# Attention stages of a two-block fp32 transformer kernel: modulation units, PSUM banks, tiles and start times of the heads rearranged

## The chip, the cores and the metric

The kernel runs on 1 core of a Trainium2 chip as one launch. The metric is device time in microseconds (us): the median of several runs. Each run is one execution of the whole program. A difference of some 0.2% (2.5 us) is what a measurement of this kernel can tell from none.

## The reference

Sequence 256, width 1024, batch 1, all in float32. A first block (modulated by a conditioning vector c) is followed by a second one of two layers. What matters of them here:

```python
# first block
mods = silu(c) @ w_ada + b_ada          # nine vectors of 1024: shift, scale, gate x 3
h += 0.5 * gate0 * rmsnorm(swiglu(modulate(rmsnorm(h), shift0, scale0)))        # d_ff 2816
p = modulate(rmsnorm(h), shift1, scale1) @ w_in    # qa ka va | qi ki wi | qb kb vb
oa = rmsnorm(dsa_sparse_attention(qa, ka, va, qi, ki, wi, rel_bias))   # 8 heads of 64, top 64 keys
ob = rmsnorm(stick_breaking_attention(qb, kb, vb))                     # 8 heads of 64
h += gate1 * rmsnorm(concat(oa, ob) @ w_out)
h += 0.5 * gate2 * rmsnorm(swiglu(modulate(rmsnorm(h), shift2, scale2)))
# second block, layer 0
h += diff_attention(rms_norm(h))     # rope, 8 heads: softmax(q1 k1) - lam * softmax(q2 k2), times v
h += sq_relu_mlp(rms_norm(h))        # d_ff 4096
# second block, layer 1
ckv = rms_norm(h) @ w_dkv;  c = rms_norm(ckv[:256]);  k_nope, v = split(c @ w_ukv)
q = rms_norm(rms_norm(h) @ w_dq) @ w_uq       # latent 384, then 8 heads of 128 + 64 (rope)
h += softmax((q_nope k_nope + q_rope k_rope) * scale) v @ w_o
h += sq_relu_mlp(rms_norm(h))
return rms_norm(h)
```

`mods` 6 and 7 are the shift and scale of the third sublayer, the second feed-forward of the first block.

## The kernel before

**Weights as one stream.** All weights come from one array, in an order that `stream_plan` writes out and the host packs accordingly. One load of SyncE's queue brings a 1 MB chunk of two units of 128x1024 (512 KB each) into one of NR = 5 raw slots. `feed()` goes down the plan. It splits a weight unit into a high fp32r part `whi` (ScalarE, L325) and the rest `wlo` (VectorE, L326), in one of NS = 5 slots, and stops when none is free. A raw slot is loaded again when both its units are used up. A unit named `ada` is a piece of `w_ada`: VectorE multiplies it with silu(c) and sums along the row in one instruction (L304), straight from the raw slot, and TensorE has nothing to do with it. `spread(units, mods, wide)` strews the 8 `ada` units of each listed modulation among the units of a stage, `wide` giving the rate.

**Products.** Each product of two float32 operands is three fp32r matmuls on TensorE (high by high, high by low, low by high). `block_T` (through `products`, whose matmuls are L363) makes one unit 24 matmuls of 128x256; `rows_times` makes it 12 of 128x512 into the four long-lived accumulators `fix` (named `pacc` in the rows). Four more PSUM banks (named `ps`) go round by `banks.take()` and `banks.give()`. Both lists are first in, first out.

**Attention beside projections.** While TensorE works through a projection, `Side` runs other parts as Python generators in between: a part issues the instructions up to its next `yield` on all engines. `nudge()` is one turn: it advances one part that is due, or begins one whose condition holds, if fewer than 5 are active. In the first block's `in_t` loop (20 units) and in the `qk` loop of the second block (16 units) a turn comes after 6 matmuls and one at the unit's end, 4 a unit. In the `uq` loop (12 blocks of 9 matmuls) one comes after each 3 matmuls. `yield n` asks for at least n turns before the next step (a bare `yield` 4, in the `uq` loop 3). `step()` is a turn with no product beside it. Every engine takes its instructions in the order in which this Python program wrote them: TensorE stands still at a head's matmul until its operand is there, whatever products stand behind it.

The parts are: `index_part` (the selection of 64 keys: 8 score heads, then 8 rounds of max and match_replace on VectorE, L1001 and L1003); 8 `stick_head`s (three steps); 8 `sparse_head`s (three steps; L1023 adds the bias, L961 is the exponential in `softmax_exp`, `transpose_p` at L932 and L937, `times_v`); two `half_out`s, which normalise 512 columns of the mixed heads and turn them into four "parts" each of the operand `o1` (L1126, L1132), kept in `nhi` and `nlo`; 8 `diff_head`s (four steps) and 8 `latent_head`s (three). In the rows L373 and L376 are the two matmul helpers `put` and `put_last`. A head may begin when it is `ripe`: the projections that it needs were issued at least 2 turns ago. Rope (`roped`, two steps, L1203 to L1214) and the evacuations of queries (L1435 on ScalarE for odd blocks, L1437 on VectorE for even ones) stand beside the heads.

**Ends of the stages.** In an attention stage the four `fix` banks are added to the four round-going ones (`open_fix`). At its end they have to be back before the next product accumulates in them:

```python
        while any(b not in banks.items for b in fix):
            side.step()
        close_fix()
```

The stages after each are `out` (order 4, 5, 6, 7, 0, 1, 2, 3), `o_a` and `o_b`; their `rows_times` gives a turn after each group of three matmuls and steps the side parts until the part that it needs is there.

**The latent stage** before: products `dkv` and `dq`, norm of the kv latent (`low_norm`, L480, L474, L482), product `dkr`, first step of its rope, turning of the normed kv latent (`turn`, L502; parts at L522, L525), second step of the rope, norm of the q latent, products `ukn`, turning of q, products `ukv`, then the `uq` loop with the heads.

## Time and profile before

| | us |
|---|---|
| median of 3 runs | 1258.34 (1258.27 to 1260.52) |
| the profiled execution | 1263.49 |
| its span | 1262.2 |
| TensorE busy in it | 1180.5 (94%), 7782 matmuls |
| VectorE / ScalarE busy | 805.5 (64%) / 619.1 (49%) |
| granted TensorE clock, mean | 0.975 |
| moved by the DMA queues | 231.78 MB, mean 184 GB/s |

How to read it: the profiled execution is 5.15 us above the median and its span 3.9 us above. A clock of 1.00 in a row is 2.4 GHz, 0.50 is 1.2 GHz. Line numbers (L363) are those of the listing. In the trace the stages lie so, in us from the span's start: start 0 to 44.8; first feed-forward 44.8 to 231; value and index projections to 281; `in_t` loop with heads 281 to 384.6; `out` product 395.7 to 426; second feed-forward 435 to 629; `qk` loop with heads 659 to 738; `o_a` to 765; MLP 774 to 950; latent stage 958 to 1045; `o_b` to 1070; MLP 1074 to 1250.

### The profile page before, as it was taken

The page shows a single profiled execution, that of the slowest core. Times are in us where ns is not written, and L with a number is a line of the kernel's source. Part 1 is how long each engine was busy: PE and PEld are TensorE (multiplying, and loading weights), DVE is VectorE, ACT ScalarE, POOL GpSimd, SP SyncE. Part 2 cuts the span into 40 slices and gives each one's busy share as a digit, 9 for nine tenths or more (in the row PEclk, how much of TensorE's full clock was granted, in tenths as well). Part 3 has the DMA queues.
Part 4 walks back from the last instruction along what each step waited for, and adds up shares of the span by engine and source line. Part 5 has one row for each costly group of instructions (what it writes and reads, how often), then busy time and mean ns, then how long its engine had stood idle before and what let it go on. Part 6 is the DMA issues. An engine that isn't in the chain of part 4 may idle for free.

```text
span 1262.2 us, 19662 instructions
## 1 busy us (share of the span) xinstructions
PE 1180.5 (94%) x7782; PEld 1084.0 (86%) x7782; DVE 805.5 (64%) x1343; ACT 619.1 (49%) x1096; POOL 59.1 (5%) x75
## 2 busy tenths in 40 slices
PE   1899999998897999999999889999999879999998
PEld 1799989898896899999989878999998767999997
DVE  6877766659654665655558876565557554655554
ACT  4444454634464544444555545445456443554453
POOL 4000000000000000000002210000000000000000
PEclk8899999989898999999999999999999899999999
DMA  9888777265431366565442223555554304455540
GB/s 382 349 349 302 278 265 266 100 234 203 156 110 67 118 235 221 211 234 184 151 170 102 102 100 133 200 173 196 188 181 173 126 35 150 144 190 194 175 165 34
DMA packets 34011, 231.78 MB, mean 184 GB/s; under 512 B 3704, under 2 KB 5120, under 8 KB 6528
## 3 DMA queue, kind: packets, MB, share of 16 engines
q1 hardware_dynamic: 31952, 226.24, 49.2%
q10 hardware_dynamic: 1968, 4.29, 1.0%
q8 instruction: 62, 1.02, 0.3%
q14 instruction: 29, 0.24, 0.1%
HBM read 229.45 MB, written 1.06 MB: 183 GB/s over the span
## 4 chain that ended last, share of the span: by engine, by line
PE 78%; DVE 13%; ACT 6%; issue 1%; POOL 1%; DMA 1%; DVEq 0%; SPq 0%; ACTq 0%; POOLq 0%
PE ps L363 37%; PE pacc L363 35%; DVE wlo L326 3%; ACT wk L961 2%; DVE raw L304 2%; ACT whi L325 1%; POOL st L468 1%; DVE st L956 1%; PE ps L376 1%; PE pacc L373 1%; PE ps L373 1%; PE pacc L500 1%; PE ps L500 1%; DVE tmp L637 1%; DMA cst<-in_const 1%
## 5 line engine op out<-in xcount | busy, mean ns | idle before, releaser
L326 DVE TENSOR_TENSOR wlo<-raw,whi 128x1024 fp32r<-128x1024 f32 x353 | 430.5, 1225 | 204.6 <-ACT whi L325 198.5
L325 ACT ACTIVATE whi<-raw 128x1024 fp32r<-128x1024 f32 x353 | 369.6, 1054 | 167.6 <-PE pacc L363 91.6
L363 PE MATMUL ps<-nhi,whi 128*128 128x256 f32 x1376 | 399.2, 290 | 20.2 <-DVE wlo L326 17.6
L363 PE MATMUL ps<-nhi,wlo 128*128 128x256 f32 x1376 | 392.3, 285 | 0.0
L363 PE MATMUL ps<-nlo,whi 128*128 128x256 f32 x1376 | 392.3, 285 | 0.0
L363 PEld LDWEIGHTS ps<-nhi,whi 128*128 128x128 f32 x1376 | 266.8, 194 | 26.8 <-ACT whi L325 19.1
L363 PEld LDWEIGHTS ps<-nlo,whi 128*128 128x128 f32 x1376 | 266.8, 194 | 5.0 <-issue 1.0
L363 PEld LDWEIGHTS ps<-nhi,wlo 128*128 128x128 f32 x1376 | 266.6, 194 | 0.0
L363 PE MATMUL pacc<-whi,hhi 128*128 128x512 f32 x440 | 173.1, 393 | 1.1 <-ACT sg L704 1.1
L363 PE MATMUL pacc<-wlo,hhi 128*128 128x512 f32 x440 | 172.5, 392 | 0.0
L363 PE MATMUL pacc<-whi,hlo 128*128 128x512 f32 x440 | 171.2, 389 | 0.0
L704 ACT ACTIVATE sg<-ps 128x256 f32<-128x256 f32 x108 | 41.5, 384 | 180.6 <-PE ps L363 180.4
L363 PEld LDWEIGHTS pacc<-whi,hlo 128*128 128x128 f32 x440 | 82.6, 188 | 18.1
L363 PEld LDWEIGHTS pacc<-whi,hhi 128*128 128x128 f32 x440 | 83.0, 189 | 16.8 <-ACT sg L704 1.4
L363 PEld LDWEIGHTS pacc<-wlo,hhi 128*128 128x128 f32 x440 | 83.0, 189 | 13.1
L706 DVE TENSOR_TENSOR hm<-sg,ps 128x256 f32<-128x256 f32 x108 | 45.4, 421 | 76.4 <-ACT sg L704 76.3
L304 DVE SCALAR_TENSOR_TENSOR raw<-raw,silu_c 128x1024 f32<-128x1024 f32 x72 | 87.7, 1226 | 0.0
L710 DVE TENSOR_TENSOR hlo<-hm,hhi 128x256 fp32r<-128x256 f32 x108 | 45.9, 425 | 52.2 <-ACT hhi L709 52.2
L709 ACT ACTIVATE hhi<-hm 128x256 fp32r<-128x256 f32 x108 | 45.1, 418 | 65.2 <-DVE hm L706 65.2
L468 POOL TENSOR_TENSOR st<-st,mod 128x1 f32<-128x1 f32 (+1 forms) x40 | 25.8, 646 | 1079.7 <-DVE st L658 429.2
L363 PE MATMUL pacc<-whi,nhi 128*128 128x512 f32 (+1 forms) x144 | 57.3, 398 | 7.1 <-DVE nlo L1132 4.3
L363 PE MATMUL pacc<-wlo,nhi 128*128 128x512 f32 (+1 forms) x144 | 55.0, 382 | 0.0
(272 smaller groups left out, 1382.8 us busy)
## 6 DMA issues: line engine op xcount, KB each, us to landing
raw<-in_stream SPq DMA_DIRECT2D x213, 1024.0 KB, 4.9
gates<-in_g_post ACTq DMA_DIRECT2D x3, 512.0 KB, 11.9
h<-in_x SPq DMA_DIRECT2D x1, 1024.0 KB, 7.3
cst<-in_const ACTq DMA_DIRECT2D x1, 1024.0 KB, 8.0
arena<-bias_rows ACTq DMA_DIRECT2D x1, 1024.0 KB, 8.2
out<-tmp SPq DMA_DIRECT2D x4, 256.0 KB, 2.1
silu_c<-in_c_row ACTq DMA_DIRECT2D x1, 512.0 KB, 5.9
arena<-in_final_g SPq DMA_DIRECT2D x1, 512.0 KB, 5.7
```

What stands on the lines that cost most here:

```text
L304: t = dve.do(lambda e: e.scalar_tensor_tensor(src, src, 1.0, silu_c[:, :], ALU.mult, ALU.mult, accum_out=adac[:, 8 * m + k:8 * m + k + 1]) ...
L325: t_hi = act.do(lambda e: e.activation(whi[:, s, :], src, ACT.Copy), arrived, room)
L326: t_lo = dve.do(lambda e: e.tensor_tensor(wlo[:, s, :], src, whi[:, s, :].bitcast(F32), ALU.subtract), arrived, room, t_hi)
L363: return e.matmul(o, lt[a], rh[b], start=start and first, stop=stop and last)
L373: pe.quiet(lambda e: e.matmul(o, lt, rh, start=start, stop=stop), *after)
L468: return pool.do(lambda e: e.tensor_tensor(r, v, ex, ALU.pow), t, t_zero)
L500: tok[c] = pe.do(lambda e: e.matmul(o, a, dg[:, i, :], start=True, stop=True), t, held[c].free)
L704: t = act.do(lambda e: e.activation(sg[:, s, :], up if gate is None else gate, ACT.Relu if gate is None else ACT.Silu), tk)
L706: t = dve.do(lambda e: e.tensor_tensor(hm[:, s, :], sg[:, s, :], up, ALU.mult), t)
L709: t1 = act.do(lambda e: e.activation(hhi[:, s, :], hm[:, s, :], ACT.Copy), t, hid["free"][s])
L710: t2 = dve.do(lambda e: e.tensor_tensor(hlo[:, s, :], hm[:, s, :], hhi[:, s, :].bitcast(F32), ALU.subtract), t1, hid["free"][s])
L961: toks.append(act.do(lambda e: e.activation(dst.ap[:, a:a + w], src[:, a:a + w], ACT.Exp, bias=mx[:, i:i + 1], accum_out=sm[:, i:i + 1]), ...
```

## The change

1. **Stream.** The 16 units of modulations 6 and 7 leave the `in_t` stretch and join modulations 2 to 5 in the first feed-forward (48 there in place of 32, at a rate of 1.03 in place of 1.1).
2. **Banks.** `retire` takes the `fix` banks out of the round one by one: one that is in hand leaves at once, one that is lent out goes to `leaving` and drops out when it is given back. It is called two units before the end of the `in_t` loop, at the last pair of the `qk` loop and three blocks before the end of the `uq` loop. The loops at the ends step only while `leaving` isn't empty.
3. **Tiles.** Parts 4 to 7 of `o1` get tiles of their own: `mhi`/`mlo` 0 to 2 and `hhi`/`hlo` 0. The half that makes them may now begin when the 8 stick heads are issued and the keys selected, where it needed all 20 projections issued (`nhi` and `nlo` hold the projections' operand until then).
4. **Start of heads.** `ripe` asks for 4 turns in place of 2, and the waits in `index_part` are 3 turns in place of 2.
5. **Last rope** of the `qk` loop becomes a side part.
6. **Latent stage.** The kv latent is normed before `dq` and turned before `dkr`, both norms stand ahead of `dkr`, and `dkr`'s rope is ended within `ukn`. A latent head's own query block must be ripe too.

```diff
-    ffn0 = spread(ffn("ffn0_", DFF // P, ("gate", "up")), (2, 3, 4, 5), 1.1)
+    ffn0 = spread(ffn("ffn0_", DFF // P, ("gate", "up")), (2, 3, 4, 5, 6, 7), 1.03)
...
-    plan += spread([("in_t", j) for j in IN_ORDER], (6, 7))
+    plan += [("in_t", j) for j in IN_ORDER]
...
+    def retire(self, rooms):
+
+        for room in rooms:
+            if room in self.items:
+                self.items.remove(room)
+            else:
+                self.leaving.append(room)
...
                 rooms.give(rl, *t_s)
                 if hh % 2:
-                    yield 2
+                    yield 3
...
-                yield 2
+                yield 3
...
         def ripe(*js):
-            return all(j in t_q and side.now - born[j] >= 2 for j in js)
-
-        o1 = Parts(nhi, nlo)
+            return all(j in t_q and side.now - born[j] >= 4 for j in js)
+
+        o1 = Parts(nhi, nlo, {4: (mhi[:, 0, :], mlo[:, 0, :]), 5: (mhi[:, 1, :], mlo[:, 1, :]),
+                              6: (mhi[:, 2, :], mlo[:, 2, :]), 7: (hhi[:, 0, :], hlo[:, 0, :])})
...
-        side.add(half_out(512, 4, t_b, 4096), lambda: len(t_b) == 8 and len(t_q) == len(IN_ORDER))
+        side.add(half_out(512, 4, t_b, 4096), lambda: len(t_b) == 8 and len(t_sel) == 2)
         side.add(half_out(0, 0, t_a, 5120), lambda: len(t_a) == 8 and 7 in o1.t)
         for n, j in enumerate(IN_ORDER):
+            if n == len(IN_ORDER) - 2:
+                banks.retire(fix)
...
-        while any(b not in banks.items for b in fix):
+        while banks.leaving:
             side.step()
-        close_fix()
...
             for g in (0, 8):
+                if hh == 7:
+                    banks.retire(fix if g == 0 else [])
...
-        t_q[pend[0]], born[pend[0]] = next(pend[1]), side.now
-        while any(b not in banks.items for b in fix):
+
+        def last_rope(at, rope):
+            t_q[at], born[at] = next(rope), side.now
+            yield
+
+        side.add(last_rope(*pend))
+        while banks.leaving:
             side.step()
-        close_fix()
...
         done_kv = low("dkv", 2, n1, 4, T, fix[0:2])
+        t_ckv = low_norm(done_kv, fix[0:2], T, 0)
         done_q = low("dq", 4, n2, 2, 384, fix[2:4])
-        t_ckv = low_norm(done_kv, fix[0:2], T, 0)
+        ckv, cq = Parts(hhi, hlo), Parts(mhi, mlo)
+        part_scaled(turn(tmp[:, :, 0:T], 2, t_ckv), [(ckv, lambda c: col("kv_g", c))])
+        t_cq = low_norm(done_q, fix[2:4], 384, 512)
...
-        ckv, cq = Parts(hhi, hlo), Parts(mhi, mlo)
-        part_scaled(turn(tmp[:, :, 0:T], 2, t_ckv), [(ckv, lambda c: col("kv_g", c))])
-        t_kr = next(rope)
-        t_cq = low_norm(done_q, fix[2:4], 384, 512)
...
                 n = 4 * f + g
+                if n == 1:
+                    t_kr = next(rope)
...
-            side.add(latent_head(hh), lambda hh=hh: hh in t_qn and ripe(hh // 2))
+            side.add(latent_head(hh), lambda hh=hh: hh in t_qn and ripe(8 + hh, hh // 2))
...
         for n, blk in enumerate(UQ_ORDER):
+            if n == len(UQ_ORDER) - 3:
+                banks.retire(fix)
...
             if blk < 8:
+                born[8 + blk], t_qr[8 + blk] = side.now, []
```

(The `uq` loop's end has the same two lines in place of three.)

**What moves, on VectorE, in the `in_t` stretch** (the selection's rounds; `wlo` is the split of a weight unit, `raw,adac` an `ada` unit). Before:

```order
L1003 MATCH_REPLACE hm<-st,hm 128x256
L326 TENSOR_TENSOR wlo<-raw,whi 128x1024
L304 SCALAR_TENSOR_TENSOR raw,adac<-raw,silu_c 128x1024
L1001 MAX st<-hm 128x8 x2
L1003 MATCH_REPLACE hm<-st,hm 128x128
L1003 MATCH_REPLACE hm<-st,hm 128x256
L1001 MAX st<-hm 128x8 x2
L1003 MATCH_REPLACE hm<-st,hm 128x128
L1003 MATCH_REPLACE hm<-st,hm 128x256
L912 TENSOR_SCALAR arena<-ps 64x256
L326 TENSOR_TENSOR wlo<-raw,whi 128x1024
L304 SCALAR_TENSOR_TENSOR raw,adac<-raw,silu_c 128x1024
```

and of the changed program, where line numbers are 11 to 13 higher:

```order
L337 TENSOR_TENSOR wlo<-raw,whi 128x1024
L1014 MAX st<-hm 128x8 x2
L1016 MATCH_REPLACE hm<-st,hm 128x128
L1016 MATCH_REPLACE hm<-st,hm 128x256
L925 TENSOR_SCALAR arena<-ps 64x256
L337 TENSOR_TENSOR wlo<-raw,whi 128x1024
L1014 MAX st<-hm 128x8 x2
L1016 MATCH_REPLACE hm<-st,hm 128x128
L1016 MATCH_REPLACE hm<-st,hm 128x256
L1060 SCALAR_TENSOR_TENSOR wk<-ps,wk 128x384
L337 TENSOR_TENSOR wlo<-raw,whi 128x1024
L1014 MAX st<-hm 128x8 x2
```

The `ada` rows are gone from between the splits and the rounds, and a split is followed by one round where two stood.

**What moves, on TensorE, at the end of the `in_t` stretch** (behind the last projection; `selr,identr` opens the logits of a sparse head, `arena,wk` is its product with the values, `dg,tmp` turns the first normed half, `pacc<-whi` is the `out` product). Before:

```order
L373 MATMUL ps<-selr,identr 128x384
L373 MATMUL ps<-arena 128x128
L376 MATMUL ps<-arena 128x256
L373 MATMUL ps<-selr,identr 128x384
L373 MATMUL ps<-arena 128x128
L376 MATMUL ps<-arena 128x256
L373 MATMUL ps<-arena,wk 128x64 x2
L376 MATMUL ps<-arena,wk 128x64
L373 MATMUL ps<-arena,wk 128x64 x2
L376 MATMUL ps<-arena,wk 128x64
L1126 MATMUL ps<-dg,tmp 128x128 x2
L363 MATMUL pacc<-whi,nhi 128x512
```

Now:

```order
L384 MATMUL ps<-arena,wk 128x64 x2
L387 MATMUL ps<-arena,wk 128x64
L384 MATMUL ps<-selr,identr 128x384
L384 MATMUL ps<-arena 128x128
L387 MATMUL ps<-arena 128x256
L384 MATMUL ps<-selr,identr 128x384
L384 MATMUL ps<-arena 128x128
L387 MATMUL ps<-arena 128x256
L1140 MATMUL ps<-dg,tmp 128x128 x2
L374 MATMUL pacc<-whi,mhi 128x512
L374 MATMUL pacc<-wlo,mhi 128x512
L374 MATMUL pacc<-whi,mlo 128x512
```

The product reads its new tiles and no longer stands behind the values' products of both last heads; the logits of two sparse heads still stand behind the last projection and ahead of it.

**What moves, on ScalarE, at the start of the `uq` stretch** (`arena<-ps` at L1435, now L1460, is the evacuation of an odd query block; `wk,st` at L961, now L974, are the exponentials of a head). Before:

```order
L1203 ACTIVATE sg<-ps 128x256
L961 ACTIVATE wk,st<-ps,st 128x128
L961 ACTIVATE wk,st<-ps,st 128x256
L325 ACTIVATE whi<-raw 128x1024
L1435 ACTIVATE arena<-ps 128x256
L961 ACTIVATE wk,st<-pacc,st 128x128
L961 ACTIVATE wk,st<-pacc,st 128x256
L1203 ACTIVATE sg<-pacc 128x256
L937 ACTIVATE wk<-pacc 128x384
L937 ACTIVATE wk<-ps 128x384
```

Now:

```order
L1218 ACTIVATE sg<-ps 128x256
L336 ACTIVATE whi<-raw 128x1024
L1460 ACTIVATE arena<-ps 128x256
L974 ACTIVATE wk,st<-ps,st 128x128
L974 ACTIVATE wk,st<-ps,st 128x256
L1218 ACTIVATE sg<-pacc 128x256
L974 ACTIVATE wk,st<-pacc,st 128x128
L974 ACTIVATE wk,st<-pacc,st 128x256
L950 ACTIVATE wk<-pacc 128x384
L336 ACTIVATE whi<-raw 128x1024
L950 ACTIVATE wk<-ps 128x384
```

The first odd query block is evacuated ahead of all exponentials, and the second head's exponentials stand before the transposed probabilities (L937, now L950) of the first.

## Rows read from the trace of the kernel before

**Rows 1.** Windows by stage; first feed-forward, in_t with tail, qk, latent.

```profile
core 0: us, PE busy (x) PEld busy (x) DVE busy (x) ACT busy (x) POOL busy (x), PEclk, DMA share, GB/s
...
44.84:231.00 186.16, 186.16 (x1286) 172.85 (x1287) 132.78 (x179) 86.02 (x119) 0.00 (x0) 0.99 0.78 292
281.00:396.00 115.00, 98.37 (x722) 94.41 (x721) 81.36 (x199) 61.55 (x139) 1.09 (x2) 0.93 0.44 155
659.00:740.00 81.00, 72.88 (x539) 68.36 (x538) 64.38 (x162) 41.80 (x123) 18.72 (x22) 0.99 0.30 105
975.00:1047.00 72.00, 57.45 (x352) 50.22 (x351) 41.31 (x94) 30.27 (x80) 5.80 (x9) 0.95 0.27 95
```

**Rows 2.** Waits of PE, 281 to 400: us in total, times, longest us.

```profile
PE ps L932 <- ACT wk L961: 4.9, 2, 4.4
PE pacc L363 <- DVE nlo L1132: 4.3, 1, 4.3
PE ps L373 <- DVE arena L912: 2.9, 2, 2.3
PE ps L1126 <- DVE wk L1023: 1.9, 1, 1.9
PE ps L373 <- ACT whi L325: 0.8, 1, 0.8
PE pacc L373 <- ACT whi L325: 0.7, 1, 0.7
```

**Rows 3.** Waits of PE, qk loop, 660 to 742.

```profile
PE pacc L373 <- DVE arena L1212: 4.2, 5, 1.1
PE pacc L363 <- DVE sg L1208: 2.4, 1, 2.4
PE ps L373 <- DVE arena L1212: 1.5, 2, 1.1
```

**Rows 4.** Waits of PE, latent stage, 975 to 1047.

```profile
PE pacc L373 <- ACT arena L1435: 5.8, 4, 2.0
PE pacc L363 <- ACT wk L961: 1.8, 1, 1.8
PE ps L373 <- DVE arena L1437: 1.6, 2, 1.2
PE ps L934 <- DVE wk L1401: 1.6, 2, 0.8
PE ps L363 <- ACT tmp L480: 0.9, 1, 0.9
```

**Rows 5.** Windows in which the clock was low: in_t, its tail, qk, latent.

```profile
308.20:311.40 3.20, 3.20 (x14) 3.02 (x14) 3.17 (x14) 2.40 (x5) 0.00 (x0) 0.50 0.40 100
340.90:345.60 4.70, 4.70 (x23) 4.70 (x24) 2.88 (x5) 2.21 (x6) 0.00 (x0) 0.50 0.34 94
390.20:400.10 9.90, 5.56 (x17) 4.42 (x18) 3.09 (x13) 3.00 (x11) 0.00 (x0) 0.50 0.14 59
738.60:741.50 2.90, 2.85 (x7) 2.28 (x8) 2.77 (x5) 0.00 (x0) 0.00 (x0) 0.50 0.00 0
980.20:983.90 3.70, 3.70 (x19) 3.70 (x20) 2.34 (x8) 0.70 (x3) 1.09 (x2) 0.54 0.01 2
1004.70:1007.80 3.10, 3.10 (x15) 2.92 (x14) 1.06 (x4) 1.14 (x5) 0.00 (x0) 0.51 0.68 222
```

**Rows 6.** Windows, early in the first feed-forward.

```profile
50.00:75.00 25.00, 25.00 (x178) 23.53 (x177) 21.69 (x29) 12.07 (x16) 0.00 (x0) 1.00 1.00 404
```

**Rows 7.** Groups by line, 44.84 to 231, VectorE.

```profile
L304 DVE SCALAR_TENSOR_TENSOR raw<-raw,silu_c 128x1024 f32<-128x1024 f32 x31 | 37.8, 1219 | 0.0
```

**Rows 8.** Waits of PE, first feed-forward, 45 to 240.

```profile
PE ps L363 <- ACT whi L325: 1.3, 1, 1.3
```

**Rows 9.** Windows, one head's period in the qk loop.

```profile
708.74:719.75 11.01, 9.93 (x75) 9.42 (x76) 8.78 (x24) 5.86 (x18) 2.65 (x3) 1.00 0.27 96
```

**Rows 10.** Groups by line, 281 to 396, VectorE.

```profile
L1028 DVE RECIPROCAL st<-st 128x2 f32<-128x2 f32 x8 | 1.3, 166 | 9.0 <-ACT wk L961 9.0
```

More of the change, by code:

```diff
@@ L142, in __init__ @@
     def __init__(self, items):
-        self.items = list(items)
+        self.items, self.leaving = list(items), []
     def take(self):
@@ L149, in give @@
         room.free = list(after)
-        self.items.append(room)
+        if room in self.leaving:
+            self.leaving.remove(room)
+        else:
+            self.items.append(room)
+    def retire(self, rooms):
+        for room in rooms:
+            if room in self.items:
+                self.items.remove(room)
+            else:
+                self.leaving.append(room)
 class Side:
@@ L1129, in mixed @@
                 k = chunk + c
-                hi, lo, o, s = nhi[:, k, :], nlo[:, k, :], b.ap[:, 0:T], col("out_g", k)
+                (hi, lo), o, s = o1.rows(k), b.ap[:, 0:T], col("out_g", k)
                 t1 = act.do(lambda e: e.activation(hi, o, ACT.Copy, scale=s), tk)
@@ L1446, in build @@
             side.nudge()
-        while any(b not in banks.items for b in fix):
+        while banks.leaving:
             side.step()
-        close_fix()
         done = rows_times([("o_b", k) for k in range(8)], range(8), o2, None, True, side.nudge)
```

8 lines of the change are left out of this document (5 added, 3 removed).

## The prediction

> **What bounds the kernel now.** I read the windows by stage first [rows 1]. In the first feed-forward TensorE is busy for all of 186.16 us: nothing is to be had there, and nothing may be lost. The three attention stretches are different: 16.6 of 115.0 us idle from 281 to 396, 8.1 of 81.0 in the `qk` stretch, 14.6 of 72.0 in the latent stage, together 39.3 us, while neither VectorE nor ScalarE is full in any of them. So latency binds there, not work: TensorE, in program order, stands at a head's matmul whose operand is late, with ready products behind it.
>
> The list of waits says which operand. From 281 to 384 they are 4.9, 2.9, 0.8 and twice 0.7 (one row stands), 10.0 us; behind the last projection come 1.9 and 4.3 us [rows 2]. In the `qk` loop a head's logits wait for its own rope, 4.2 + 1.5 us in seven waits, and `o_a` waits 2.4 us for the last rope [rows 3]. In the latent stage 5.8 us go to query blocks that ScalarE has not evacuated, 1.6 to those of VectorE, 1.8 to exponentials that hold a bank, 1.6 to the turning of probabilities, and 0.9 with two more of 0.8 to the norm of the kv latent [rows 4].
>
> The last view is the granted clock in short windows [rows 5]. Behind TensorE's idle time it stands at 0.50 (1.2 GHz) for 3.20 and 4.70 us of busy time in the `in_t` loop, 5.56 behind the gap of its tail, 2.85 behind the `qk` loop, 3.70 and 3.10 in the latent stage. Work there takes twice as long, so half of it is lost: 1.6 + 2.35, 2.8, 1.4, 1.85 + 1.55 us. If the waits go, these go with them.
>
> **The change, part by part.**
>
> *The 16 modulation units, arriving.* An `ada` unit costs VectorE 1219 ns [rows 7]; 16 are 19.5 us, and its busy time in the first feed-forward goes from 132.8 to 152.3 of 186.2 us, 82% [rows 1]. Is that hidden? From 50 to 75 us VectorE was busy for 21.69 of 25 us (87%) and TensorE still for all 25.00, with 404 GB/s from memory [rows 6]. The new stretch needs 292 GB/s [rows 1] plus 8.4 MB in 186 us, 337. So both resources have been seen above what is asked. I charge one more wait of the size of the one that stands there, 1.3 us [rows 8]; the ends are 0 and, if nothing were covered, 19.5. If the cover goes, the splits are late, and the whole stage with them. The Trainium skill, "DMA: Bandwidth & Descriptors", section "Specifications", gives about 358 GB/s as a core's limit from HBM. By it the sum would stay, since 337 is below, but only by 6%; the trace disagrees with it as a ceiling (404, rows 6).
>
> *The same units, leaving.* SyncE's queue gets 8 loads of 1 MB less in the `in_t` stretch; 155 GB/s show that it does not bind there, so this part is worth nothing. VectorE loses a 1.2 us instruction behind each split; a head's or the selection's step standing behind one came that much later.
>
> *Heads wait four turns, selection three.* TensorE's waits on freshly made operands (2.9, 0.8, 0.7, 0.7 in `in_t`) are shorter, each but one, than the two turns of 6 matmuls that are added: 75 matmuls in 9.93 us [rows 9] make 12 of them 1.6 us. The 4.9 us are mostly one wait of 4.4 us on a head's exponentials, whose VectorE input stood behind a split and an `ada` unit. With the unit gone and the selection's rounds thinned out I take all 10.0 us as gained, and 3.95 of clock. What is late next: the sparse heads, which begin later, crowd the end of the loop. I charge three new waits of 0.8 us (the commonest size in rows 2), ends 0 and 10.0. In the tail, by the order, the two last heads still stand behind the last projection and ahead of the first product that uses the new tiles. Their VectorE work is unchanged, so 4.3 and 1.9 us stay, but for the 0.5 us that a values' product moved behind. Sum: 10.0 + 3.95 + 0.5 − 2.4 = **12.0 us**.
>
> *The qk stretch.* Seven waits for rope, 5.7 us, vanish by the two turns, but not to full profit. In a head's period of 11.01 us VectorE works 8.78 us [rows 9], and its rest are waits within the head's own chain. The period stays; the two turns shift projections ahead once, 1.5 us. `o_a` no longer stands behind the last rope: 2.4 us, and 1.4 of clock. Added wait: with the long banks retired at the last pair, the round has as few as four banks, and a head takes two at once. The nearest row is the bank held by exponentials, 1.8 us [rows 4]; ends 0 and, with one for each of the two last heads, 3.6. Behind that matmul on TensorE is the last projection, for which the last head waits. Sum: 1.5 + 2.4 + 1.4 − 1.8 = **3.5 us**.
>
> *The latent stage.* The kv norm now runs under the `dq` products: 2.5 us. The first odd query block is evacuated ahead of the exponentials on ScalarE, and a head begins only when its block is ripe: 5.8 + 1.6 + 1.8 = 9.2 us. The 1.6 us on the turning of probabilities stay: that chain is as long as before. Clock: 3.4 us. New waits: again three of 0.8. Ends: 0 and 9.2, if the turns only move the wait from logits to probabilities. Sum: 2.5 + 9.2 + 3.4 − 2.4 = **12.7 us**.
>
> *Banks that retire singly and the early first half.* Neither has a row of its own: the loops that they shorten end in the tail, where the heads decide. I put both at nothing beyond what is counted, since every stage's sum has its bank wait.
>
> **Sum.** 12.0 − 1.3 + 3.5 + 12.7 = 26.9 us. The profiled execution, 1263.49, would come to 1236.6; the median of runs lies 5.15 lower, so **1231.4 us**. Its own range: without any of the new waits (6.6 us) 1225, with the charges doubled (7.9 us, all four) 1239.
>
> **The rivals.**
>
> *(a) The chains bind, and half of it is gained.* VectorE waits 9.0 us on exponentials in eight sparse heads [rows 10], 1.1 each, and no turn changes that. In the `qk` loop this rule holds; it may hold in the others. Then of the 4.9 us two `ada` units' worth goes (2.4) and 2.5 stays, with 2.35 of its clock; in the latent stage half of the 5.8 stays, the 1.8, and 1.55 of clock (6.25); in `qk` the 1.5 fail. 26.9 − 4.85 − 6.25 − 1.5 = 14.3: **1244**. Against it: in the latent stage VectorE works 41.3 and ScalarE 30.3 of 72 us [rows 1].
>
> *(b) The tail closes too.* If the early half and its own tiles free the path to the first `out` product, 4.3 + 1.9 − 0.5 = 5.7 us and 2.8 of clock come on top: **1222.9**. Against it: the order, where the two heads keep their place, and a `nlo` of VectorE is what the product waits for.
>
> *(c) The first feed-forward turns VectorE- or stream-bound.* Nearly two in three units there would carry an `ada` unit, as early in that stretch, but for longer. At worst all 19.5 us come out on the path in place of 1.3: **1249.6**. Rows 6 speak against it.
>
> *(d) Slower: too few banks.* From the call of `retire` on, 8 turns and 2 units in `in_t`, 8 and 2 in `qk`, 9 and 3 blocks in `uq` share ever fewer banks, down to four, where eight went round. That is up to some 30 takes. A take that finds its bank held costs what the waits on held banks or tail operands show: 1.9, 2.4, 1.8 us [rows 2 to 4], 2.0 in the mean. With 13 such waits the gain is eaten; with 15, 3 us are lost: about **1261**. For it: the round is first in, first out, so one late head blocks all. Against it: a turn is 0.8 us or less, and the heads' chains give back a bank after each exponential. The Trainium skill, "TensorE: Matmul & The Clock Gate", section "A second HAM failure mode: psum-queue depth-cycling", describes TensorE idling briefly at PSUM banks that go round, with a clock that swings. What the trace has of it is the six low-clock windows [rows 5], all in stretches where banks go round; none is in the first feed-forward, with 0.99.
>
> **How the numbers follow.** The forecast gets 0.46: its rows are explicit, but three terms hang on "all waits go". (a) 0.28, (b) 0.10, (c) 0.08, (d) 0.08. The range 1221 to 1250 takes in the forecast, (a), (c) and most of (b), and leaves out (d) and the ends of the others. Faster by over 0.2% (2.5 us) are the first four but for stragglers, 0.91. (d) is split: 0.05 within 0.2% with what strays from (c), 0.04 slower.
>
> **What would show it.** In the changed profile: the first feed-forward still about 186 us, TensorE full, VectorE near 82%. The stretch from the first `in_t` product to the last about 12 us shorter, with no wait above 2 us and the clock at 1.00. Then a gap of some 10 us before `out`, as now. In `qk` no wait on a rope, the period still about 11 us, one wait on a bank at the end. In the latent stage no wait on L1435's successor and less than 5 us of waits in all. The prediction is wrong in its main part if waits on exponentials or turned probabilities add up to over 5 us in the `in_t` or `uq` loop (a), if `out` starts within 5 us of the last projection (b), if the first feed-forward is longer by over 4 us (c), or if waits on banks add up to over 10 us (d).

## The result, and the profile after

The changed kernel ran at 1246.51 us in the median of 4 runs (1245.58 to 1250.12), the one before at 1259.43 in the same comparison: a ratio of 0.9898, 95% interval 0.9868 to 0.9927. It is faster by 12.9 us, 1.0%; 27 were forecast. The profiled execution took 1246.54 us with a span of 1245.2, mean clock 0.982.

Windows by stage of the kernel before, cut at its own first and last products: in_t stretch (first `in_t` product to first `out` product), qk stretch (first `qk` product to the end of `o_a`), latent stage (first `dq` product to the end of `o_b`). The columns are the busy times of PE, PEld, DVE, ACT, POOL, then the clock, the DMA share and GB/s.

```profile
274.93:395.71 120.78, 104.15 (x749) 100.19 (x750) 84.87 (x207) 63.33 (x143) 1.64 (x3) 0.91 0.42 151
655.90:767.48 111.58, 103.46 (x699) 94.31 (x698) 83.43 (x197) 56.45 (x157) 20.10 (x24) 0.98 0.33 115
964.99:1069.95 104.96, 90.41 (x524) 79.46 (x523) 59.62 (x113) 46.64 (x103) 5.80 (x9) 0.97 0.33 116
```

The same of the changed kernel. Ahead of them stands a stretch of its first feed-forward, cut at the times of rows 1 and not at its own products:

```profile
core 0: us, PE busy (x) PEld busy (x) DVE busy (x) ACT busy (x) POOL busy (x), PEclk, DMA share, GB/s
44.84:231.00 186.16, 186.16 (x1302) 172.83 (x1301) 150.25 (x213) 84.19 (x118) 0.00 (x0) 1.00 0.89 337
271.06:384.08 113.02, 100.59 (x744) 96.75 (x744) 70.26 (x178) 63.23 (x143) 1.64 (x3) 0.94 0.29 103
645.72:765.55 119.83, 105.53 (x699) 96.98 (x698) 86.88 (x197) 55.19 (x157) 17.82 (x24) 0.97 0.30 107
963.06:1053.03 89.97, 85.59 (x524) 77.16 (x523) 58.75 (x113) 45.87 (x103) 5.90 (x9) 1.00 0.38 135
```

The first feed-forward is as forecast: TensorE full in all of these 186.16 us, VectorE at 150.25 (81%), 337 GB/s. The in_t stretch is 7.8 us shorter, 113.0 for 120.8. The latent stage is 15.0 us shorter, 90.0 for 105.0. But the qk stretch is **8.3 us longer**, 119.8 for 111.6, where 3.5 less were forecast. Of these 8.3 us, 6.2 are idle time of TensorE (14.3 for 8.1 us), the other 2.1 busy time, at a clock of 0.97 for 0.98.

Waits of PE in the changed kernel's qk stretch (645 to 766; us in total, times, longest), which answer to [rows 3]:

```profile
PE ps L1302 <- DVE wk L1297: 7.8, 4, 2.5
PE pacc L1302 <- DVE wk L1297: 5.4, 3, 1.9
...
PE ps L384 <- DVE arena L1227: 0.4, 1, 0.4
```

The waits on the rope (5.7 us in rows 3) are down to 0.4. In their place TensorE waits in seven of the eight heads, 13.2 us in all, at L1302. That is a head's last matmul: it normalises the head's output by a diagonal that VectorE makes at L1297. The view of before has no such wait at the matching line L1287.

Waits in the in_t stretch (272 to 384) and behind it, for [rows 2]:

```profile
PE pacc L384 <- DVE selr L1024: 3.1, 1, 3.1
PE ps L945 <- ACT wk L974: 1.8, 2, 1.0
PE ps L1140 <- DVE st L487: 0.6, 1, 0.6
PE ps L1140 <- DVE dg L501: 0.5, 1, 0.5
```

```profile
PE pacc L374 <- DVE mlo L1146: 5.5, 1, 5.5
```

The gap before `out` stands at 11.9 us (11.1 before); the forecast kept it too, but for 0.5 us less. Within the stretch one new wait of 3.1 us has come up: the first sparse head stands on TensorE before VectorE has finished the selection. In the latent stage (984 to 1026, rows 4) the waits on query blocks are gone but for one, which is a wait for a bank:

```profile
PE ps L947 <- DVE arena L1462: 1.7, 1, 1.7
```

A second new wait lies ahead of this window, in `ukn`. The waits on the kv latent's norm are gone there, but TensorE stands at the third product until a copy on VectorE (L1082) has freed a bank. That copy stands behind the norm of the q latent and the 1.21 us split of a unit:

```profile
979.18 0.39 PE L374 MATMUL ps<-hhi,whi 128*128 128x256 f32 x1 [1.61 <-DVE arena L1082]
```

### The profile page after: what moved, and what is told of

Same layout as the page of the kernel before. It is cut to its first block, busy times and chain, and to the rows that moved or that the text cites. A ratio compares the mean times of both kernels' runs of the same rounds, so it can differ in the third digit from the quotient of the medians.

```text
span 1245.2 us, 19659 instructions
## 1 busy us (share of the span) xinstructions
PE 1172.4 (94%) x7782; PEld 1079.5 (87%) x7782; DVE 807.0 (65%) x1343; ACT 615.2 (49%) x1096; POOL 57.0 (5%) x75
## 4 chain that ended last, share of the span: by engine, by line
PE 82%; DVE 11%; ACT 4%; issue 1%; POOL 1%; DMA 1%; DVEq 0%; SPq 0%; ACTq 0%; POOLq 0%
PE ps L374 39%; PE pacc L374 35%; DVE wlo L337 2%; ACT wk L974 2%; PE ps L384 2%; DVE raw L315 1%; PE ps L387 1%; PE pacc L384 1%; POOL st L481 1%; ACT whi L336 1%; DVE st L969 1%; PE pacc L387 1%; PE pacc L513 1%; PE ps L513 1%; DVE tmp L650 1%
## 5 line engine op out<-in xcount | busy, mean ns | idle before, releaser
L337 DVE TENSOR_TENSOR wlo<-raw,whi 128x1024 fp32r<-128x1024 f32 x353 | 430.2, 1224 | 191.4 <-ACT whi L336 186.1
L374 PE MATMUL ps<-nhi,whi 128*128 128x256 f32 x1392 | 404.8, 291 | 19.6 <-DVE wlo L337 17.2
L374 PEld LDWEIGHTS pacc<-whi,hhi 128*128 128x128 f32 x444 | 83.8, 189 | 16.9 <-ACT sg L717 1.4
L374 PEld LDWEIGHTS pacc<-wlo,hhi 128*128 128x128 f32 x444 | 83.8, 189 | 13.2
L374 PE MATMUL pacc<-whi,nhi 128*128 128x512 f32 (+1 forms) x128 | 49.7, 388 | 1.2 <-DVE n2lo L539 0.5
L374 PE MATMUL pacc<-whi,nlo 128*128 128x512 f32 (+1 forms) x128 | 48.2, 376 | 0.0
## 6 DMA issues: line engine op xcount, KB each, us to landing
gates<-in_g_post ACTq DMA_DIRECT2D x3, 512.0 KB, 13.7
```

What stands on the lines that cost most here:

```text
L337: t_lo = dve.do(lambda e: e.tensor_tensor(wlo[:, s, :], src, whi[:, s, :].bitcast(F32), ALU.subtract), arrived, room, t_hi)
L374: return e.matmul(o, lt[a], rh[b], start=start and first, stop=stop and last)
```

## Why seven new waits: VectorE's queue in one head's period

VectorE in the kernel before, one head's period (start us, duration, line, operation; in brackets the idle time ahead and what ended it):

```profile
713.43 0.35 DVE L1264 TENSOR_SCALAR wk<-wk,st 128x256 f32<-128x256 f32 x1
713.81 0.48 DVE L1266 SCALAR_TENSOR_TENSOR wk<-wk,st 128x256 f32<-128x256 f32 x1
714.21 0.16 DVE L474 TENSOR_SCALAR st<-st 128x2 f32<-128x2 f32 x1
715.18 0.42 DVE L1279 COPY wk<-pacc 128x256 f32<-128x256 f32 x1 [0.80 <-POOL st L468]
715.52 0.73 DVE L1282 TENSOR_SCALAR wk<-cst,st 128x128 f32<-128x128 f32 x2
```

VectorE in the changed kernel, the same place in a head's period:

```profile
708.99 0.49 DVE L1281 SCALAR_TENSOR_TENSOR wk<-wk,st 128x256 f32<-128x256 f32 x1
709.40 0.42 DVE L1223 TENSOR_TENSOR sg<-pacc,cst 128x256 f32<-128x256 f32 x1
709.85 0.87 DVE L1229 TENSOR_TENSOR arena<-sg,hm 64x256 f32<-64x256 f32 x2
710.75 1.23 DVE L337 TENSOR_TENSOR wlo<-raw,whi 128x1024 fp32r<-128x1024 f32 x1
711.89 0.16 DVE L487 TENSOR_SCALAR st<-st 128x2 f32<-128x2 f32 x1
712.86 0.43 DVE L1294 COPY wk<-ps 128x256 f32<-128x256 f32 x1 [0.80 <-POOL st L481]
713.20 0.71 DVE L1297 TENSOR_SCALAR wk<-cst,st 128x128 f32<-128x128 f32 x2
```

The norm of a head's output is a small chain: squares on ScalarE, the mean at L487 on VectorE (L474 before), a power on GpSimd, then the diagonal (L1297, before L1282). Before, L474 stood right behind the last step of the next head's difference of probabilities (L1266), and the diagonal was there 2.0 us later. Now a whole rope (L1223, L1229) and the 1.23 us split of a weight unit (L337) stand between. ScalarE had the squares ready by 708.8, yet L487 ran at 711.89. TensorE, in order, stood at L1302 until 713.97, 1.76 us, and the next head's logits and all products stood behind it. No instruction was added: two turns of delay moved the heads' third step past a `feed()` in program order.

The same chain can be read in every run, from the timelines of ScalarE, VectorE and TensorE. Each row has the second to the fifth head; times are in us and counted from the end of a head's squares:

| | L487 begins | TensorE reaches L1302 | wait at L1302 |
|---|---|---|---|
| kernel before | 1.16 to 1.17 | 3.94 to 3.95 | 0 |
| run 1, 2 turns | 1.16 to 1.18 | 3.94 to 3.95 | 0 |
| run 2, 3 turns | 3.04 to 3.15 | 3.38 to 3.57 | 1.54 to 1.84 |
| changed, 4 turns | 3.06 to 3.15 | 3.37 to 3.53 | 1.60 to 1.85 |
| run 4 | 3.06 to 3.15 | 3.37 to 3.38 | 1.75 to 1.85 |
| run 3, 5 turns | 1.29 | 2.70 to 2.75 | 0.62 to 0.67 |
| run 13 | 1.29 to 3.18 | 2.75 to 4.75 | 0 to 2.42 |

The wait follows L487 and not the number of turns. In the fourth head the diagonal is there 5.1 us behind the squares where it was 3.2 before, and TensorE comes 3.4 us behind them where it came 3.9: 1.9 us of the shift are VectorE's, 0.6 are TensorE's.

## The experiments

All but run 11 are built from the changed kernel, and what isn't named is as in it. A stretch is cut in each run at its own first and last products, read from TensorE's timeline. Times are medians of 4 runs (9 in the seventh, a single one in the tenth and the eleventh), ratios against the kernel before on the same chip.

**1. Two turns in the qk stretch.** `ripe` reads its number from a variable that is 2 in this stretch:

```diff
-            return all(j in t_q and side.now - born[j] >= 4 for j in js)
+            return all(j in t_q and side.now - born[j] >= turns[0] for j in js)
...
         side = Side(5)
+        turns[0] = 2
         born.clear()
```

> The changed kernel, but a diff_head may begin after 2 turns again; everything else (16 units moved, banks retired singly, own tiles, last rope as a side part, latent stage) as changed. Theory A (the loss of the qk stretch comes from the phase: with 4 turns the norm of a head's output stands on VectorE behind a rope and a 1.2 us split, so TensorE waits 1.8 us at L1302 in each head): those seven waits, 13.2 us, vanish, waits on the rope of some 5 us come back, and the stretch from the first qk product to the end of o_a, 119.8 us in the changed kernel and 111.6 before, falls to 108 to 111: total 8 to 11 us below the changed kernel, about 1237. Rival B (the retired banks or the last rope are to blame): the stretch stays above 117 us, total within 2 us of the changed kernel.

1238.14 us, ratio 0.9825 (0.9809 to 0.9840), 8.4 us below the changed kernel. Its qk stretch took 112.9 us. Waits of PE there:

```profile
PE pacc L384 <- DVE arena L1227: 3.1, 4, 1.1
PE ps L384 <- DVE n2lo L539: 2.7, 1, 2.7
PE ps L1302 <- DVE wk L1297: 1.8, 1, 1.8
PE ps L384 <- DVE arena L1227: 1.5, 2, 1.1
```

VectorE in a head's period, L487 right behind L1281 again:

```profile
709.91 0.48 DVE L1281 SCALAR_TENSOR_TENSOR wk<-wk,st 128x256 f32<-128x256 f32 x1
710.31 0.16 DVE L487 TENSOR_SCALAR st<-st 128x2 f32<-128x2 f32 x1
...
711.61 0.73 DVE L1297 TENSOR_SCALAR wk<-cst,st 128x128 f32<-128x128 f32 x2
```

Seven waits at L1302 have become one, the rope's are back (4.6 us). Of theory A and rival B, A held, though the stretch lies 1.9 us above the 108 to 111 that A had. The wait of 2.7 us on `n2lo` is for a bank that a head's last step holds (run 12, without retiring, has none): the price of retiring banks, for which the forecast had set 1.8. So with the order of before the stretch is still 1.3 us longer than before.

**2. Three turns.** As the first, with `turns[0] = 3`.

> As the run with 2 turns in the qk stretch, but with 3. VectorE's order in a head's period is the same as with 4 turns (the norm behind a rope and a split). Theory A: the waits at L1302 stay, over 10 us in all, total within 2 us of the changed kernel (1246). Rival C (it is the number of turns by which heads start later, each costing its own time): about half of the loss comes back, some 4 us, about 1242.

1244.47 us, ratio 0.9874 (0.9835 to 0.9914), the runs scattered from 1238.30 to 1249.22. The median is halfway between A's figure and C's, so the time decides nothing; the two short runs have the higher clock (0.987 and 0.988, the others 0.979). The trace decides. Waits in the qk stretch:

```profile
PE ps L1302 <- DVE wk L1297: 8.5, 6, 1.8
PE pacc L1302 <- DVE wk L1297: 3.6, 2, 1.8
```

Eight waits, 12.1 us: with VectorE's order as in the changed kernel they are as there, and the stretch takes 118.0 us. One turn less than in the changed kernel bought next to nothing.

**3. Five turns.** With `turns[0] = 5`.

> As before with 5 turns. Heads start later still, but on VectorE the norm now stands behind only half a rope (0.8 us) and no split. Theory A: the waits at L1302 shrink to under 5 us in all and the total falls by 4 to 8 us, 1239 to 1243. Rival C (later heads cost by themselves): total 2 us or more above the changed kernel, 1248 or more.

1238.06 us, ratio 0.9823 (0.9807 to 0.9840). Heads begin later than in the changed kernel, and the stretch is the shortest so far, 110.7 us. The waits at L1302 are still seven, but short:

```profile
PE ps L1302 <- DVE wk L1297: 2.7, 3, 1.2
PE pacc L1302 <- DVE wk L1297: 2.5, 4, 0.6
```

Rival C (later heads cost by themselves) falls here.

**4. TensorE comes later to the last step.**

```diff
-            yield
+            yield 5
             b = banks.take()
             for i in range(2):
                 tk = pe.do(lambda e: e.matmul(b.ap[:, i * P:i * P + P], ov.ap
...
```

> The changed kernel with 5 turns asked between a head's product with the values and its last step, where 4 were (the last yield of diff_head). VectorE's order in a period is unchanged, TensorE comes to L1302 6 matmuls (0.8 us) later. Rival D (TensorE simply comes too early): each wait shrinks from 1.8 to 1.0 us, 5 to 6 us off in all, 1241. Theory A (the chain through VectorE sets the head's period, TensorE only has its idle time there): the idle time moves to another matmul and the total stays within 2 us of 1246.

1244.94 us, ratio 0.9883 (0.9869 to 0.9898), the stretch 117.8 us, and the waits at L1302 11.2 us in seven. But the edit did not do what was expected of it. TensorE's timeline has 30 projection matmuls, five turns, between a head's product with the values and L1302, in the `qk` loop of the changed kernel and of this run alike: asking for five turns changed nothing there, only the two last heads' waits beside `o_a` (1.4 and 0.8 us for 1.8 and 2.5). So this run does not test rival D. Run 3 does: with 30 matmuls there too TensorE comes earlier, 2.7 us behind the squares where it was 3.4, and waits 0.6 us and not 1.8. D explains at most the 0.6 us in the table's reading above.

**13. Four turns kept, the product with the values two turns later.**

```diff
             pt, t = transpose_p(x0, ts)
-            yield
+            yield 6
             b, tk = times_v(pt, [vd[:, i, P * hh:P * hh + P] for i in range(2)], P, t, t_v)
```

> The changed kernel, 4 turns kept, with 6 turns in place of 4 between the turning of a diff_head's probabilities and its product with the values. This alone puts the norm on VectorE behind half a rope (0.8 us) and no longer behind a whole rope and a 1.2 us split, with the beginnings of the heads where the change has them. Theory A (what stands ahead of the norm on VectorE is the loss): waits at L1302 under 6 us in all where they were 13.2, the stretch from the first qk product to the end of o_a 111 to 115 us where it was 119.8, median 1238 to 1242. Rival E (4 turns before a head begins are the loss, whatever the order): within 2 us of 1246.5 or above, since heads end later still.

1239.42 us, ratio 0.9835 (0.9813 to 0.9858), the stretch 111.0 us. Waits at L1302:

```profile
PE ps L1302 <- DVE wk L1297: 4.8, 3, 2.4
...
PE pacc L1302 <- DVE wk L1297: 0.8, 2, 0.6
```

5.6 us in five. Heads begin where the change has them, and 7.1 us are back. The order was not healed in every head, as had been expected: a split still stands right ahead of L487 in several of them, as here:

```profile
709.73 1.22 DVE L337 TENSOR_TENSOR wlo<-raw,whi 128x1024 fp32r<-128x1024 f32 x1
710.87 0.16 DVE L487 TENSOR_SCALAR st<-st 128x2 f32<-128x2 f32 x1
```

But the squares come at another place in that order, and L487 follows them sooner, at 1.5 us in this head. In the head where it takes 3.18 us, TensorE waits 2.42. With runs 1 to 3 this shows the cause: how long the norm stands in VectorE's queue, not when a head begins.

**5. The modulation units back in the in_t stretch.** The first two hunks of the change's diff undone (the stream plan).

> The changed kernel with its 16 modulation units back in the in_t stretch (stream plan of before), all else as changed. The prediction's step: in the first feed-forward they cost 1.3 us at most, in the in_t stretch they stood ahead of the heads' steps, worth some 2 to 4 of its 10 us of waits. So the time to the first in_t product stays within 2 us, the stretch from there to the first out product grows by 2 to 5 us from 109 to 113, total 1248 to 1251. Rival: VectorE's place in the in_t stretch was not short, and the turns alone took the waits: total within 2 us of 1246.5.

1251.77 us, ratio 0.9935 (0.9917 to 0.9953), 5.3 above the changed kernel. The in_t stretch took 117.2 us, and the first `in_i` product came at 267.77 us; in the changed kernel at 265.73, but in runs 4, 7, 8, 12 and 15, which have its stream plan, between 267.1 and 267.6 (the clock was at 0.69 from 45 to 50 us in run 15, at 1.00 in the changed kernel's profile). The kernel before has 267.53, with a clock of 0.50 from 45.2 to 48.6. So the 16 units cost nothing that could be measured in the first feed-forward. Their absence is worth 4 to 5 us in the stretch: 117.2 us lie 4.0 above the longest and 5.5 above the mean of the nine executions compared at the end of this text, though the intervals of the two ratios overlap. The wait on the selection was 5.7 us here:

```profile
PE pacc L384 <- DVE selr L1024: 5.7, 1, 5.7
```

**6. Two turns in the in_t stretch.** `turns` starts at 2, the index part's waits are 2 again.

> The changed kernel with 2 turns in the in_t stretch (ripe at 2, the index part's waits at 2), 4 in the other two. The prediction's step: these turns take most of the waits of 10 us in the in_t stretch, so 3 to 6 us come back: total 1249 to 1252. Rival: as in the qk stretch, it is the order on VectorE that counts and the moved units did the work, total within 2 us of 1246.5 or below it.

1250.65 us, ratio 0.9928 (0.9909 to 0.9948), 4.1 above; the stretch took 115.2 us. By the medians the turns carry 4 us there and the units 5, but this interval too overlaps the changed kernel's (0.9868 to 0.9927). The stretch is 2.0 us above the longest of the nine executions and 3.5 above their mean.

**7. Two turns in the latent stage.** The condition is `ripe(hh // 2)` with 2 turns, as before.

> The changed kernel with 2 turns in the latent stage and without the head's wait for its own query block (as before), all else as changed. From uq's first product to o_b's first 35.0 us in the changed kernel, 51.0 before. The prediction's step: the waits for unevacuated blocks, 5.8 + 1.6 us, and the clock behind them come back: 43 us or more in that stretch, total 1254 to 1257. Rival: it is the banks that retire singly, and the stretch stays under 38 us, total 1246 to 1249.

1256.05 us, ratio 0.9967 (0.9957 to 0.9977), 9.5 above: the largest part of the whole. From uq's first product to `o_b`'s first went 49.4 us (35.0 in the changed kernel); the `o_b` product behind it was shorter, 24.9 us for 28.5. Waits of PE, 975 to 1042:

```profile
PE pacc L384 <- ACT arena L1461: 3.8, 3, 2.0
PE ps L947 <- DVE wk L1423: 1.9, 3, 0.8
PE ps L384 <- DVE arena L1463: 1.6, 2, 1.2
PE ps L384 <- ACT arena L1461: 1.6, 1, 1.6
```

The waits on query blocks are back, 5.4 us on ScalarE's and 1.6 on VectorE's, as in rows 4, although banks retire singly and the kv latent is turned early.

**8. The long banks waited for together.** The three calls of `retire` gone, the three ends as before the change.

> The changed kernel with the four long banks waited for together at the ends of the three stretches, as before, and no early retiring. The prediction put this part at nothing but new bank waits. By that the total stays within 2 us of 1246.5, with the gaps before out, o_a and o_b unchanged (11.9, 0.1, 0.4 us). Rival: it is what closes the gaps: those before o_a and o_b open again to 3 to 5 us each and the total is 1249 to 1254.

1242.46 us, ratio 0.9850 (0.9822 to 0.9878), the runs from 1237.88 to 1246.05. The gap before `o_b` stayed closed (0.4 us), that before `out` opened by 1.0, that before `o_a` by 1.5, and yet both loops got shorter: `qk` 83.8 us for 86.2, `uq` 32.6 for 34.6. Most of the first is the clock (0.98 for 0.96): TensorE's idle time in the `qk` loop is 9.4 us for 10.0. The second has a clock of 1.00 in both, and the wait of 1.7 us at L947 is gone. The interval meets that of the changed kernel, so the total alone is not clear; run 15 takes it up.

**9. Parts 4 to 7 back in the old tiles.**

```diff
-        o1 = Parts(nhi, nlo, {4: (mhi[:, 0, :], mlo[:, 0, :]), 5: (mhi[:, 1, :], mlo[:, 1, :]),
-                              6: (mhi[:, 2, :], mlo[:, 2, :]), 7: (hhi[:, 0, :], hlo[:, 0, :])})
+        o1 = Parts(nhi, nlo)
...
-        side.add(half_out(512, 4, t_b, 4096), lambda: len(t_b) == 8 and len(t_sel) == 2)
+        side.add(half_out(512, 4, t_b, 4096), lambda: len(t_b) == 8 and len(t_q) == len(IN_ORDER))
```

> The changed kernel with parts 4 to 7 back in nhi and nlo, and the half that makes them begun only once all 20 projections are issued, as before. The prediction's step: own tiles change nothing but 0.5 us, because two sparse heads stand behind the last projection either way. So the gap before the out product stays at 11 to 12.5 us and the total within 2 us of 1246.5. Rival (the prediction's case b turned round): the early half saves its share and the gap grows by 2 us or more.

1248.37 us, ratio 0.9901 (0.9878 to 0.9924), gap 11.9 us: nothing that can be told, as the forecast had it.

**10. The kv latent's norm and turning back behind `dq` and `dkr`**, and the end of `dkr`'s rope ahead of `ukn`, as before.

> The changed kernel with the kv latent's norm and turning back behind dq and dkr. From dq's end to ukv's first product 12.3 us in the changed kernel and 15.1 before; from dkv to dq and all else unchanged. The prediction's step (2.5 us of waits plus 1.85 of clock): the way from the first dq product to ukv grows from 20.9 to 23 to 25.5 us. Rival: it stays under 22 us.

One execution: 1249.60 us. From dq's first product to ukv's first went 23.3 us, in the changed kernel 20.9, and 20.9 in the others that share its order too. This part is worth 2.4 us; the forecast had 2.5 of waits and 1.85 of clock.

**11. The kernel before once more.**

> The kernel before, unchanged, profiled a second time. The first profiled execution lay 5 us above the median of its runs, and the prediction carried this offset over to the changed kernel, whose profiled execution lay at its median. If the offset is a matter of where the clock falls in one execution, this one differs from the first (1262.2 us) by some us, in the attention stretches alone, with the same waits and fewer or more windows at the low clock; if it is the profiler's, the profiled execution is again 4 to 6 us above the median.

1259.72 us, span 1258.4, its runs' median being 1259.81. The first profiled execution, 3.8 us longer, differs from it in two places and in the clock alone. The clearest is the index projection, 49 matmuls in both; first execution, then second:

```profile
267.53:274.93 7.40, 7.40 (x49) 7.39 (x48) 5.38 (x11) 2.34 (x5) 0.55 (x1) 0.70 0.98 382
```

```profile
267.56:272.83 5.27, 5.27 (x49) 5.27 (x48) 4.74 (x8) 2.17 (x5) 0.00 (x0) 1.00 0.98 378
```

2.1 us lie here, 1.5 in the in_t loop.

**12. Two turns in `qk` and the banks together everywhere.**

> The changed kernel with both parts undone that the runs showed to cost: diff heads begin after 2 turns, and the long banks are waited for together in all three stretches. If the two gains (8.4 us and 4.0 us in the medians) are separate, the median is 1234 to 1236, 24 to 26 below the kernel before. If the bank part was noise of the clock, 1237 to 1239.

1238.32 us, ratio 0.9824 (0.9805 to 0.9844): as the first run. In the qk stretch the banks' gain did not add (114.3 us for 112.9, the gap before `o_a` at 3.5 again), in the latent stage it did (`uq` 33.0 us). In the qk stretch this run differs from the kernel before only in the last rope's place. The loop is as before (79.2 us), but the stretch is 2.7 us longer: `o_a` waits 3.1 us for the rope (2.4 before), and a new wait of 1.7 us stands at L1301, the last matmul of a head. The last rope as a side part, from which the forecast had 3.8 us, brought nothing here.

**14. The first sparse head five turns behind the selection.**

```diff
+            born["sel"] = side.now
...
-            side.add(sparse_head(hh), lambda hh=hh: ripe(hh // 2, 4 + hh // 2) and len(t_sel) == 2)
+            side.add(sparse_head(hh), lambda hh=hh: ripe(hh // 2, 4 + hh // 2) and len(t_sel) == 2 and side.now - born['sel'] >= 5)
```

> The changed kernel, but the first sparse head may begin only 5 turns after the selection's last instruction was issued, so that TensorE does not come to it 3.1 us early. If that wait is what the in_t stretch lost of the forecast: no wait on the selection, the clock at 1.00 there in every execution, 3 to 5 us off, median 1242 to 1244. Rival: the delay is handed on to the heads at the end and the gap before out grows by as much, median 1246 to 1248.

1246.51 us, ratio 0.9887 (0.9863 to 0.9911): nothing. The wait on the selection is gone, and new ones stand behind the last projection, where the gap grew from 11.9 to 13.7 us:

```profile
PE pacc L374 <- DVE mlo L1147: 4.2, 1, 4.2
PE ps L1141 <- DVE wk L1037: 2.8, 1, 2.8
```

The rival held: the delay is handed on. The stretch took 109.2 us in this profile and 112.2 in that of run 16, with the same instructions in it; one execution alone would have misled.

**15. Five turns in `qk`, the latent stage's banks together.** Beside `turns[0] = 5` in the qk stretch:

```diff
-            if n == len(UQ_ORDER) - 3:
-                banks.retire(fix)
...
-        while banks.leaving:
+        while any(b not in banks.items for b in fix):
             side.step()
+        close_fix()
         done = rows_times([("o_b", k) for k in range(8)], range(8), o2, None, True, side.nudge)
```

> The changed kernel with 5 turns in the qk stretch and the long banks of the latent stage waited for together. Gains seen in profiles: 9.1 us from the first qk product to the end of o_a and 1.6 from the first uq product to the end of o_b. If they add: median 1235 to 1237. If the retiring of banks costs nothing: 1238.

1234.48 us, ratio 0.9794 (0.9776 to 0.9812), 12 us below the changed kernel and clear of it. Against run 3, from which it differs by the banks alone, the gain of 3.6 us is not quite clear (intervals 0.9776 to 0.9812 and 0.9807 to 0.9840). The qk stretch took 110.8 us, `uq` 33.0. The wait of 1.7 us at L947 for a bank is gone; the longest wait left between 975 and 1042 is this one (that of 1.6 us in `ukn` lies earlier and stays):

```profile
PE ps L384 <- DVE arena L1229: 0.4, 1, 0.4
```

**16. All three.**

> The changed kernel with 5 turns in the qk stretch, the latent stage's banks waited for together and the first sparse head 5 turns behind the selection. If all three are gains of their own: median 1231 to 1234, 25 us or more below the kernel before. If the wait on the selection is only handed on: as the run without it, 1236 to 1238.

1235.34 us, ratio 0.9794 (0.9771 to 0.9816): as the run before it. Waiting for the selection brings nothing here either.

## Why the prediction was right or wrong

It was wrong by half: 12.9 us for 27, with the sign right and the range (1221 to 1250) holding the time. That the range held it is partly luck: the latent stage gave 2.3 us more than forecast and the first feed-forward cost 1.3 less. Rival (a), 1244, came nearest to the number, but its reasons weren't what happened.

| step | forecast | measured | by |
|---|---|---|---|
| units arriving in the first feed-forward | −1.3 | 0 | profile, run 5 |
| in_t stretch | 12.0 | 7.8 | profile; units 4 to 5, turns 2 to 4 by runs 5, 6 |
| qk stretch | 3.5 | −8.3 | profile, runs 1 to 4, 13 |
| latent stage | 12.7 | 15.0 | profile; turns 9.5, kv order 2.4 by runs 7, 10 |
| offset of the profiled execution | 5.15 kept | none | run 11 |

**The qk step failed, at "The period stays; the two turns shift projections ahead once".** I had read from rows 3 and 9 which waits would go, and took the order of VectorE's work within a period as given. But turns and units interlock: 8 turns are one head, 4 are one unit, and moving a head's begin by two turns moves each of its steps to another side of a rope and a split. The order of the changed program would have shown it before any run: L487 behind L337. The cost per head was 1.6 to 1.9 us of wait on TensorE in six heads, 2.5 in the seventh. Periods of 11.0 us became 11.7 and 11.8, and 13.2 to 13.3 where the clock fell behind such a wait.

A second term of the same sum failed too: 2.4 us and 1.4 of clock for the last rope. With the order of before (run 1) the stretch is 1.3 us longer than before, and at its best (run 3) 0.9 shorter. The gap before `o_a` did close, from 3.5 to 0.1 us, but in run 1 waits of 2.7 and 1.8 us came in its place, and in run 12 the rope's new place alone, with the banks waited for together, went with 2.7 us more.

**The latent step held**, and more: the waits in its `uq` loop went as the rows said, by the turns and the wait for the head's own block (run 7). TensorE's idle time fell by 10.2 us (14.6 to 4.4), where 9.3 were forecast, its busy time by 4.8. The kv part gave less, 2.4 us for 4.35 (run 10). The charge of three new waits of 0.8 us came as two, 1.6 in `ukn` and 1.7 in the `uq` loop, both for a bank.

**The in_t step was right in mechanism, too large in size.** "I charge three new waits of 0.8 us" was the term: what came was 3.1 us on the selection and 1.8 on exponentials, and a new stretch of low clock behind the first. TensorE's idle time fell by 4.2 us (16.6 to 12.4), where the forecast had 8.1; its busy time fell by 3.6, near the 3.95 of clock that were forecast. TensorE's timeline at the wait on the selection in the changed kernel, and the window of 8 us behind it:

```profile
323.19 0.66 PE L384 MATMUL pacc<-selr,identr 128*128 128x384 f32 x1 [3.12 <-DVE selr L1024]
```

```profile
323.19:331.19 8.00, 8.00 (x41) 7.77 (x42) 4.25 (x11) 2.36 (x7) 0.00 (x0) 0.64 0.04 5
```

At 0.64 of the clock for 8.00 us of busy time, about 2.9 us are lost beside the 3.1 of the wait.

The tail kept its gap: rival (b) was rightly low. Rival (c) had nothing to it: VectorE at 81% under a full TensorE cost nothing. What the trace shows, 337 GB/s over the stage with TensorE busy in 186.16 of 186.16 us, agrees with the limit of about 358 GB/s of the Trainium skill ("DMA: Bandwidth & Descriptors", section "Specifications") as far as the mean goes; the 404 of rows 6 go beyond it. One reading behind rival (d) was wrong: the first feed-forward of the kernel before does have a low clock, 0.50 from 45.2 to 48.6 us, which a mean of 0.99 hides; and PSUM banks go round there too. Rival (d), waits on banks, happened on a small scale: in the changed kernel 0.7 us at `n2lo`, 1.7 at L947 and 1.6 in `ukn`, in run 1 2.7 at `n2lo`. Single retiring costs some 1.6 us in the latent stage (`uq` loop of runs 8, 12 and 15); in the qk stretch no gain or cost of it is shown. I had set it at nothing.

**The offset.** I subtracted 5.15 us because the profiled execution of before lay that much above its runs. It was an execution in which the clock stood low for longer (run 11); the changed kernel's profiled execution lay at its own median. Some 4 us of the 17 by which the two profiled executions differ are of this kind.

## What to carry to other kernels

Where one program order feeds several in-order engines, a delay of one thread of work is not a shift: it re-sorts every engine's queue, and a small operation that others wait for can land behind a large one that nobody awaits. Before trusting a new delay, read for one period what stands ahead of each short chain's first link on every engine, above all what is slow there. And take a profiled execution's distance from the median as noise of that execution until a second one shows it again.

## What was not expected of the hardware

Behind the same wait the clock falls in one execution and not in another. In nine executions whose instructions from the first `in_t` product to the first `out` product are the same, that stretch took 108.9 to 113.2 us, mean 111.7. The wait on the selection is 3.12 us in all nine. In six of them the matmul behind it takes 0.66 us, and the stretch 111.7 to 113.2; in the other three (runs 1, 3, 4) it takes 0.41, and the stretch 108.9 to 110.4. Of these three, run 4 has the fall a little later (0.79 over the 8 us behind the wait), and runs 1 and 3 have none. Behind it the changed kernel's profile has a clock of 0.64 (above); run 1, with the same instructions, has this, timeline and window:

```profile
321.93 0.41 PE L384 MATMUL pacc<-selr,identr 128*128 128x384 f32 x1 [3.12 <-DVE selr L1024]
```

```profile
321.93:329.93 8.00, 8.00 (x62) 7.84 (x63) 4.29 (x11) 3.16 (x10) 0.00 (x0) 1.00 0.07 16
```

At this wait 2.9 us are at stake. The nine differ at the start and at the end of the stretch as well; the whole of it has a mean clock of 0.99 in run 1 and of 0.94 in the changed kernel's profile. Single runs of one kernel lie 4 to 5 us apart here, about twice what counts as a difference, and the longer ones have the lower clock: of the changed kernel's, 0.978 at 1250.12 us and 0.983 at 1245.58. The Trainium skill describes in "TensorE: Matmul & The Clock Gate", section "A second HAM failure mode: psum-queue depth-cycling", a clock that swings where TensorE idles briefly between groups of matmuls. The traces agree in that most low windows lie behind idle time. They show besides that the same idle time need not bring one, and that one can come without it: in the changed kernel TensorE is busy in 20.90 of the 20.90 us up to 270.9, and the clock is 0.51 in the 3.5 us that follow.
